# Split weights with a low half by GpSimd, in place of unsplit weights, for twelve projection tiles a layer

## The chip, the cores and the metric

The kernel runs on one core of a Trainium2 chip. The time is the device time of one execution in microseconds (us), lower is better. Matrices are multiplied by TensorE, elementwise work is done by VectorE, ScalarE and GpSimd, and the weights are read from device memory by transfers that the queue of SyncE issues.

## The reference

Two blocks of a network run one after the other, each of two layers, on 256 tokens of width 1024 in fp32. The first block's layer is

```
z = rmsnorm(x) @ w_in + b_in         # val, glu, gates, pool input, q, k, v, indexer q and k
conv  = silu(layernorm(depthwise 31-tap conv(val * sigmoid(glu)))) @ pw
pool  = windowed means of pin, mixed by small matrices
attn  = softmax over the top 64 keys an indexer picks, per query, 8 heads of 64
y     = concat(conv, pool, attn) * silu(gates)
x     = x + y @ w_out                # then a gated per-layer embedding
```

The second block (gated linear attention, short convolution, neighbourhood attention, a feed-forward part of width 2816, on 256 tokens and 256 context tokens) takes most of the time; the change doesn't touch it.

## The kernel before

**Weights.** All large weights come as a stream of units of 128x1024 fp32, in the order of use, each by one transfer into a ring `RAWB` of four slots (L457). A product in full fp32 precision is mostly made of three products of reduced precision: ScalarE writes the rounded high half of a unit into `WHI` (L1488), VectorE writes the rest, `RAWB - WHI`, into `WLO` (L2092), both rings of `SPL` = 3. TensorE's `fm` then does, for each of the eight 128x128 slabs, high weight by high x, high weight by low x, low weight by high x (L590 to L592): 24 products of 128x128 weights and 256 tokens a tile. Both engines convert units two ahead of use (`AHEAD`): in each tile's step they first convert the unit of the tile two further on and then go to the tile's own work.

**The stretch in question.** In each layer of the first block 25 projection tiles (`TILES1`) follow each other. Tiles 0 to 12 are done as told. Tiles 13 to 24 (`kb`, `pin`, `agate`, `cgate`, `pgate`) are "native" before the change: `native` (L596 to L609) multiplies the fp32 slot of `RAWB` as it is by the fp32 normalised x in `Y1`. One such product is two instructions in the trace, so a tile is 16 of them (L606). These units are not split: `NATIVE` marks them, `split_to` of ScalarE and VectorE passes over them, `SPLIT_NO` and `SPLIT_W` number the others, and the slot of `RAWB` is free when TensorE is done with it (`unit_done`).

**What lies beside these tiles.** The order on each engine is written out by hand; every engine runs its own program and waits for the others on semaphores. While the tiles go through TensorE, VectorE does rotations (`rope`), the selection of the 64 keys by repeated maxima (`topk`), the 31 taps of the convolution (`taps`, L2315, in pairs of two channel halves, after each pair a wait on its own semaphore), and per attention item (`attend`, eight items from tile 14 on) a masked maximum of each of two heads (L2338), a negation (L2342) and a reciprocal (L2348). ScalarE adds the bias on the way out of the bank (`Z`), takes the exponentials, scales them and copies the turned weights (`PT`). TensorE makes scores, turns the weights and multiplies them by the values after each tile's products. At tile 23 TensorE takes the convolution's channel mean (L1066), which needs all taps; VectorE's subtraction of it (L2359), ScalarE's square and the variance follow.

**GpSimd** does nearly nothing in this block: some transfers of its own (one, the context, waits for tile 17's eviction) and waits.

Of the kernel before, what the change touches and what calls it, by code (L numbers as in the profile page):

```python
# [19 lines left out]
F32 = mybir.dt.float32  # L20
F32R = mybir.dt.float32r
ALU = mybir.AluOpType
# [4 lines left out]
P = 128  # L27
# [19 lines left out]
    ["pin"] * 2 + ["agate"] * 4 + ["cgate"] * 2 + ["pgate"] * 2  # L47
Z1 = {n: TILES1.index(n) for n in TILES1}
NZ1 = len(TILES1)
NATIVE_FROM = Z1["kb"]  # L50
ATTEND_FROM = 14
ROPES1 = (("kiwi", 1), ("qi", 2), ("qa", 2), ("ka", 2), ("qb", 2), ("kb", 2))
ROTATE_AT = {2: 0, 3: 1, 9: 2, 11: 3, 13: 4, 15: 5}
# [73 lines left out]


def stream():
    widths, native, beside = [], [], []  # L130

    def add(ws, unsplit=False):
        widths.extend(ws)
        native.extend([unsplit] * len(ws))

    def rows(units):
        beside.extend([(len(widths) + AHEAD, ROW)] * units)

    def dots(units):
        beside.extend([(len(widths) + AHEAD, DOT)] * units)  # L140

    for l in range(DEPTH):
        add([UNIT] * 4)
        for t in range(NZ1):
            add([UNIT], t >= NATIVE_FROM)
            rows(2 if t in ROWS1 else 0)
        add([UNIT] * (2 + KS + KS))
    for l in range(DEPTH):
        add([2 * VGW] * 4)
        for i in range(NFIRST):  # L150
            add([UNIT])
            dots(DOTS_PROJ[i] if l == 0 else 0)
        for j, width in enumerate([2 * VW] * 4 + [UNIT] * (NZ2 - NFIRST)):
            add([width])
            dots(DOTS_PROJ[NFIRST + j] if l == 0 and NFIRST + j < len(DOTS_PROJ) else 0)
        rows(ROW_U if l == 0 else 0)
        for m in range(KS):
            add([UNIT])
            dots(DOTS_OUT[m] if l == 0 else 0)
        for m in range(2 * FT):  # L160
            add([UNIT])
            dots(l == 0 and m in DOTS_UP)
        for m in range(KS):
            add([UNIT, UNIT, 6 * P])
            dots(DOTS_DOWN[m] if l == 0 else 0)
    order = []
    for w in range(len(widths)):
        order.extend([kind for at, kind in beside if at == w] + [w])
    return widths, native, order


WIDTHS, NATIVE, ORDER = stream()
NW, NU = len(WIDTHS), len(ORDER)
W_AT = [ORDER.index(w) for w in range(NW)]
R_AT = [u for u in range(NU) if ORDER[u] == ROW]
D_AT = [u for u in range(NU) if ORDER[u] == DOT]
DOT_N = [2 if t < ROW_TILES + 4 else 1 for t in DOT_TILES for _ in range(4)]
DOTTED = [sum(DOT_N[:k]) for k in range(len(D_AT) + 1)]
SPLIT_W = [w for w in range(NW) if not NATIVE[w]]
SPLIT_NO = [sum(not x for x in NATIVE[:w]) for w in range(NW)]  # L180


def layout(names):
# [13 lines left out]
def build(nc, ws, prm, crep, cc, c1, c2, xt, ptin, mat1, wgp, nab, out):  # L197
    with ExitStack() as ctx:
# [234 lines left out]
        @block.sync  # L433
        def _(sp):

            def load_x(k):

                sp.dma_start(X[:, 2 * k:2 * k + 2, 0:T], xt[:, 2 * k:2 * k + 2, 0:T]).then_inc(S(f"ld_x{k}"), 16)

            load_x(0)  # L440
            for u in range(NU):
                if u in (1, 2):
                    load_x(u + u - 1)
                    if u == 1:
                        load_x(2)
                if u >= RAW:
                    w = ORDER[u - RAW]
                    if w == DOT:
                        sp.wait_ge(S("dot_summed"), DOTTED[D_AT.index(u - RAW) + 1])
                    elif w == ROW:  # L450
                        sp.wait_ge(S("row_done"), R_AT.index(u - RAW) + 1)
                    elif NATIVE[w]:
                        sp.wait_ge(S("unit_done"), w + 1)
                    else:
                        sp.wait_ge(S("lo_ready"), SPLIT_NO[w] + 1)
                n = UNIT if ORDER[u] < 0 else WIDTHS[ORDER[u]]
                sp.dma_start(RAWB[:, u % RAW, 0:n], ws[u, :, 0:n]).then_inc(S(f"raw{u % RAW}"), 16)  # L457
            for k in range(0, KS, 2):
                sp.wait_ge(S("x_new"), KS * (DEPTH + 1) + k + 2)
                sp.dma_start(out[:, k:k + 2, :], X[:, k:k + 2, 0:T]).then_inc(S("stored"), 16)  # L460
            sp.wait_ge(S("stored"), 16 * KS // 2)
# [3 lines left out]
        def _(pool):  # L465
# [6 lines left out]
            for l in range(DEPTH):  # L472
                if l > 0:
                    pool.wait_ge(S("x_new"), me.nth("x_new", KS))
                if l == 0:
                    pool.wait_ge(S("ms_ready"), 1)
                pool.dma_start(M1[:], mat1[l]).then_inc(S("ld_p1"), 16)
                pool.dma_start(PIN[:], ptin[l]).then_inc(S("ld_p1"), 16)
                if l == 0:
                    pool.dma_start(K1[:], c1).then_inc(S("ld_c1"), 16)  # L480
                    pool.wait_ge(S("ld_prm"), 16)
                nc.gpsimd.tensor_tensor(PB[:], prm_col(f"poolb{l}", 0, 2), prm_col(f"pools{l}", 0, 2), ALU.mult).then_inc(S("pb_ready"), 1)
                pool.wait_ge(S("z_freed"), NZ1 * l + 18)
                if l == 0:
                    pool.dma_start(X[:, :, T:TC], xt[:, :, T:TC]).then_inc(S("ld_ctx"), 16)
                pool.wait_ge(S("z_freed"), NZ1 * (l + 1))
            me.seen["z_freed"] = NZ1 * DEPTH
            pool.wait_ge(S("x_split"), me.nth("x_split", KS * DEPTH))
# [45 lines left out]
        def _(pe):  # L534
# [8 lines left out]
            def unit():  # L543

                u = me.u
                me.u += 1
                k = SPLIT_NO[u]
                pe.wait_ge(S("lo_ready"), k + 1)
                return WHI[:, k % SPL, :], WLO[:, k % SPL, :]

            def rows(b, s0=0, s1=KS, at=0, tiles=1):

# [23 lines left out]
            def fm(slabs, n, rhs, freed, given=None, given_from=0, order=None, b=None):  # L576

                b = me.next_tile() if b is None else b
                if b in held:
                    pe.wait_ge(*held[b])  # L580
                o = bank[b][:, 0:n]
                order = list(order or range(slabs))
                for i, s in enumerate(order):
                    if i % 8 == 0:
                        hi, lo = unit()
                    if given is not None and i >= given_from:
                        pe.wait_ge(S(given), me.nth(given))
                    w = slice((s % 8) * P, (s % 8 + 1) * P)
                    xh, xl = rhs(s)
                    nc.tensor.matmul(o, hi[:, w], xh, start=(i == 0), stop=False)  # L590
                    nc.tensor.matmul(o, hi[:, w], xl, start=False, stop=False)  # L591
                    ins = nc.tensor.matmul(o, lo[:, w], xh, start=False, stop=(i == slabs - 1))  # L592
                    if i % 8 == 7 and i != slabs - 1:
                        ins.then_inc(S("unit_done"), 1)
                ins.then_inc(S("unit_done"), 1)
                read_by(b, freed)  # L596

            def native(b, freed):

                if b in held:  # L600
                    pe.wait_ge(*held[b])
                u = W_AT[me.u]
                me.u += 1
                pe.wait_ge(S(f"raw{u % RAW}"), 16 * (u // RAW + 1))
                for s in range(KS):
                    ins = nc.tensor.matmul(bank[b][:, 0:T], RAWB[:, u % RAW, s * P:(s + 1) * P], Y1[:, s, :],  # L606
                                           start=(s == 0), stop=(s == KS - 1))
                ins.then_inc(S("unit_done"), 1)
                read_by(b, freed)  # L609

# [320 lines left out]
            for l in range(DEPTH):  # L931
# [165 lines left out]
                for t in range(NZ1):  # L1097
                    b = t % 4 if t < ATTEND_FROM - 1 else t % 2
                    if t < UNDIVIDED:
                        fm(KS, T, x_lat, "zr_ready", b=b)  # L1100
                        made["z_freed"] = made.get("z_freed", 0) + 1
                    elif t < NATIVE_FROM:
                        fm(KS, T, x_new, "z_freed", "x_split" if t == UNDIVIDED else None, b=b)
                    else:
                        native(b, "z_freed")
                    if t in ROWS1:
                        i = ROWS1.index(t)
                        pe.wait_ge(S("c_ready"), 1)
# [374 lines left out]
        def _(act):  # L1483
# [6 lines left out]
            def split_to(n):  # L1490

                nonlocal split
                while split < min(n, NW):
                    u, k, w = W_AT[split], SPLIT_NO[split], WIDTHS[split]
                    split += 1
                    if NATIVE[split - 1]:
                        continue
                    act.wait_ge(S(f"raw{u % RAW}"), 16 * (u // RAW + 1))
                    if k >= SPL:
                        act.wait_ge(S("unit_done"), SPLIT_W[k - SPL] + 1)  # L1500
                    A(WHI[:, k % SPL, 0:w], RAWB[:, u % RAW, 0:w]).then_inc(S("hi_ready"), 1)

            def rest(n=1):
# [574 lines left out]
        def _(dve):  # L2078
# [4 lines left out]
            def split_to(n):  # L2083

                nonlocal split
                while split < min(n, NW):
                    u, k, w = W_AT[split], SPLIT_NO[split], WIDTHS[split]
                    split += 1
                    if NATIVE[split - 1]:
                        continue  # L2090
                    dve.wait_ge(S("hi_ready"), k + 1)
                    V.tensor_tensor(WLO[:, k % SPL, 0:w], RAWB[:, u % RAW, 0:w], WHI[:, k % SPL, 0:w].bitcast(F32),  # L2092
                                    ALU.subtract).then_inc(S("lo_ready"), 1)
# [1082 lines left out]
```

## Time and profile before

| | us |
|---|---|
| runs of the kernel | 1410.52, 1406.16, 1413.89 (median 1410.52) |
| the profiled execution | 1411.34 |
| its span, first to last instruction | 1409.5 |
| TensorE busy | 1360.2 |
| VectorE busy | 1033.9 |
| ScalarE busy | 709.9 |
| GpSimd busy | 49.8 |

The mean granted clock of TensorE is 0.988 of full speed. All times of rows are microseconds from the start of the span unless marked ns. A busy time counts overlapping instructions once; TensorE's products are pipelined, so that one product's duration is longer than the distance to the next. An engine can be busy all the time without being what ends last, and the other way round.

### The profile page before, as it was taken

To read this page: it belongs to the slowest core of one execution; us is meant where nothing else is said; L and a number is where in the kernel's file an instruction comes from. 1 tells how busy PE (TensorE), PEld (TensorE's weight loads), DVE (VectorE), ACT (ScalarE), POOL (GpSimd) and SP (SyncE) were. 2 spreads that over 40 slices of the span, in tenths; PEclk is the share of its full clock that TensorE was granted. 3 is DMA by queue.
4 is the path that set the end of the run, shared out by engine and by line. 5 is a ranking of instruction groups with operands and counts; after the bars stand their busy time and mean duration, and the time that the engine had idled before them with its cause. 6 is when DMAs were issued, how large, how long until landed. Compare 5 with 4: busy or idle time off the path is not lost.

```text
span 1409.5 us, 21836 instructions
## 1 busy us (share of the span) xinstructions
PE 1360.2 (96%) x8477; PEld 1174.1 (83%) x8477; DVE 1033.9 (73%) x1951; ACT 709.9 (50%) x1205; POOL 49.8 (4%) x69
## 2 busy tenths in 40 slices
PE   6999999999999999999999999999999988999997
PEld 5777997879988886677888888888889877999997
DVE  6597786988679875766788888766653855788854
ACT  6536666367555632644443444322355645666643
POOL 1000000000010012000000000000000110000000
PEclk9999999999999999998999999999999999999999
DMA  7633556425456522141455544577533432455553
GB/s 262 233 133 112 189 183 219 141 91 179 154 191 195 165 90 102 50 137 57 136 160 166 164 153 154 175 265 249 162 117 105 135 105 67 139 185 180 180 193 107
DMA packets 61655, 217.73 MB, mean 154 GB/s; under 512 B 6992, under 2 KB 9040, under 8 KB 61168
## 3 DMA queue, kind: packets, MB, share of 16 engines
q1 hardware_dynamic: 58912, 204.76, 44.0%
q0 software_dynamic: 2496, 11.56, 2.4%
q8 instruction: 68, 1.11, 0.3%
q14 instruction: 35, 0.29, 0.1%
q10 hardware_dynamic: 144, 0.00, 0.0%
HBM read 215.25 MB, written 1.05 MB: 153 GB/s over the span
## 4 chain that ended last, share of the span: by engine, by line
PE 85%; ACT 6%; DVE 5%; issue 2%; DMA 1%; DVEq 0%; SPq 0%; ACTq 0%
PE bank L590 20%; PE bank L592 20%; PE bank L591 20%; PE bank L606 5%; ACT WHI L1488 2%; PE bank L1293 2%; DVE WLO L2092 1%; PE bank L651 1%; PE bank L653 1%; PE bank L652 1%; PE bank L628 1%; PE bank L629 1%; PE bank L630 1%; DMA RAWB<-in_ws 1%; PE bank L1435 1%
## 5 line engine op out<-in xcount | busy, mean ns | idle before, releaser
L590 PE MATMUL bank<-NHI,WHI 128*128 128x256 f32 (+1 forms) x1376 | 456.3, 332 | 7.7 <-DVE WLO L2092 6.0
L2092 DVE TENSOR_TENSOR WLO<-RAWB,WHI 128x1024 fp32r<-128x1024 f32 (+2 forms) x274 | 326.4, 1194 | 172.0 <-ACT WHI L1488 171.4
L591 PE MATMUL bank<-NLO,WHI 128*128 128x256 f32 (+1 forms) x1376 | 450.4, 327 | 0.0
L592 PE MATMUL bank<-NHI,WLO 128*128 128x256 f32 (+1 forms) x1376 | 450.4, 327 | 0.0
L1488 ACT ACTIVATE WHI<-RAWB 128x1024 fp32r<-128x1024 f32 (+2 forms) x274 | 281.7, 1031 | 175.6 <-PE bank L592 94.6
L590 PEld LDWEIGHTS bank<-NHI,WHI 128*128 128x128 f32 x1376 | 261.4, 190 | 39.4 <-issue 8.3
L591 PEld LDWEIGHTS bank<-NLO,WHI 128*128 128x128 f32 x1376 | 261.6, 190 | 23.7 <-issue 1.4
L592 PEld LDWEIGHTS bank<-NHI,WLO 128*128 128x128 f32 x1376 | 261.5, 190 | 22.7
L2187 DVE CUSTOM_DVE_ANT_0 DP<-RAWB,CREP,PRM 128x1024 f32<-128x1024 f32 x120 | 153.9, 1282 | 7.1 <-DMA RAWB<-in_ws 1.8
L1488 ACT ACTIVATE CF<-bank,PRM 128x512 f32<-128x512 f32 (+1 forms) x88 | 59.2, 673 | 179.3 <-PE bank L592 176.3
L590 PE MATMUL bank<-HHI,WHI 128*128 128x256 f32 (+1 forms) x330 | 109.4, 331 | 0.2 <-DVE WLO L2092 0.2
L592 PE MATMUL bank<-HHI,WLO 128*128 128x256 f32 (+1 forms) x330 | 109.3, 331 | 0.0
L591 PE MATMUL bank<-HLO,WHI 128*128 128x256 f32 (+1 forms) x330 | 109.3, 331 | 0.0
L606 PE MATMUL bank<-Y,RAWB 128*128 128x256 f32 x384 | 88.2, 383 | 0.0
L2918 DVE SCALAR_TENSOR_TENSOR CF<-bank,PRM,CF 128x510 f32<-128x510 f32 (+1 forms) x88 | 54.1, 615 | 46.3 <-ACT CF L1488 44.9
L606 PEld LDWEIGHTS bank<-Y,RAWB 128*128 128x128 f32 x384 | 71.5, 190 | 11.8 <-issue 2.7
L590 PEld LDWEIGHTS bank<-HHI,WHI 128*128 128x128 f32 x330 | 61.8, 187 | 7.6 <-DVE WLO L2092 0.4
L591 PEld LDWEIGHTS bank<-HLO,WHI 128*128 128x128 f32 x330 | 61.8, 187 | 7.1
L592 PEld LDWEIGHTS bank<-HHI,WLO 128*128 128x128 f32 x330 | 61.8, 187 | 7.1
L1488 ACT ACTIVATE L<-L,ST 128x256 f32<-128x256 f32 (+2 forms) x100 | 50.2, 517 | 31.0 <-DVE ST L2205 15.1
L1488 ACT ACTIVATE ZB<-bank 128x512 f32<-128x512 f32 (+1 forms) x34 | 17.4, 513 | 79.3 <-PE bank L592 79.2
L2921 DVE SCALAR_TENSOR_TENSOR CF<-bank,PRM,CF 128x510 f32<-128x510 f32 (+1 forms) x88 | 54.2, 616 | 3.1
(360 smaller groups left out, 1990.3 us busy)
## 6 DMA issues: line engine op xcount, KB each, us to landing
RAWB<-in_ws SPq DMA_DIRECT2D x362, 512.0 KB, 3.4
RAWB<-in_ws SPq DMA_DIRECT2D x24, 384.0 KB, 3.9
RAWB<-in_ws SPq DMA_DIRECT2D x8, 416.0 KB, 3.2
NB<-in_nab POOLq DMA_DIRECT2D x12, 256.0 KB, 3.4
CREP<-in_crep POOLq DMA_DIRECT2D x2, 1024.0 KB, 5.1
K<-in_c POOLq DMA_DIRECT2D x2, 896.0 KB, 5.6
K<-in_c POOLq DMA_DIRECT2D x1, 1344.0 KB, 8.6
X<-in_xt SPq DMA_DIRECT2D x4, 256.0 KB, 5.4
```

The lines of the kernel that those rows point to most:

```text
L590: nc.tensor.matmul(o, hi[:, w], xh, start=(i == 0), stop=False)
L591: nc.tensor.matmul(o, hi[:, w], xl, start=False, stop=False)
L592: ins = nc.tensor.matmul(o, lo[:, w], xh, start=False, stop=(i == slabs - 1))
L606: ins = nc.tensor.matmul(bank[b][:, 0:T], RAWB[:, u % RAW, s * P:(s + 1) * P], Y1[:, s, :], start=(s == 0), stop=(s == KS - 1))
L628: nc.tensor.matmul(o, hi[:, w], xh, start=(i == 0), stop=False)
L629: nc.tensor.matmul(o, hi[:, w], xl, start=False, stop=False)
L1293: ins = nc.tensor.matmul(bank[b][key_rows(j, c), c * P:(c + 1) * P], keys(j, c, 2 * seqs)[:, i, :], QD[:, i % 2, j, c * P:(c + 1) * P], st ...
L1488: return nc.scalar.activation(out, in_, func, **kw)
L2092: V.tensor_tensor(WLO[:, k % SPL, 0:w], RAWB[:, u % RAW, 0:w], WHI[:, k % SPL, 0:w].bitcast(F32), ALU.subtract).then_inc(S("lo_ready"), 1)
L2187: V.tensor_tensor_reduce(out=prod[:], in0=RAWB[:, u % RAW, :], in1=rep[:, c, :], scale=1.0, scalar=prm_col(f"bada{l}", at), op0=ALU.mult, ...
L2918: V.scalar_tensor_tensor(y[:, :, 1:], b[:, :, :-1], prm_col(f"fw{l}", j), y[:, :, 1:], ALU.mult, ALU.add).then_inc(S("dve_chain"), 1)
L2921: V.scalar_tensor_tensor(y[:, :, :-1], b[:, :, 1:], prm_col(f"fw{l}", 4 * FT + j), y[:, :, :-1], ALU.mult, ALU.add).then_inc(S("up_freed"), 1)
```

## The change

The twelve tiles a layer go through `fm` with split weights like the others. Their high halves are made by ScalarE, their low halves by GpSimd instead of VectorE. `NATIVE`, `SPLIT_NO`, `SPLIT_W` and `native` go away; every unit now takes a place in the rings `WHI` and `WLO`, and every slot of `RAWB` is free when the low half is made.

```diff
-NATIVE_FROM = Z1["kb"]
+POOL_FROM = Z1["kb"]
...
@@ SyncE's queue
-                    elif NATIVE[w]:
-                        sp.wait_ge(S("unit_done"), w + 1)
                     else:
-                        sp.wait_ge(S("lo_ready"), SPLIT_NO[w] + 1)
+                        sp.wait_ge(S("lo_ready"), w + 1)
...
@@ GpSimd
-                pool.wait_ge(S("z_freed"), NZ1 * l + 18)
-                if l == 0:
-                    pool.dma_start(X[:, :, T:TC], xt[:, :, T:TC]).then_inc(S("ld_ctx"), 16)
+                first = BY_POOL.index(True) if l == 0 else len(BY_POOL) - BY_POOL[::-1].index(True) - NZ1 + POOL_FROM
+                for k in range(first, first + NZ1 - POOL_FROM):
+                    if k == first + 20 - POOL_FROM:
+                        pool.wait_ge(S("z_freed"), NZ1 * l + 18)
+                        if l == 0:
+                            pool.dma_start(X[:, :, T:TC], xt[:, :, T:TC]).then_inc(S("ld_ctx"), 16)
+                    pool.wait_ge(S("lo_ready"), k)
+                    pool.wait_ge(S("hi_ready"), k + 1)
+                    nc.gpsimd.tensor_tensor(WLO[:, k % SPL, :], RAWB[:, W_AT[k] % RAW, :], WHI[:, k % SPL, :].bitcast(F32),
+                                            ALU.subtract).then_inc(S("lo_ready"), 1)
...
@@ TensorE
-                    elif t < NATIVE_FROM:
+                    else:
                         fm(KS, T, x_new, "z_freed", "x_split" if t == UNDIVIDED else None, b=b)
-                    else:
-                        native(b, "z_freed")
...
@@ ScalarE, split_to
-                    if NATIVE[split - 1]:
-                        continue
                     act.wait_ge(S(f"raw{u % RAW}"), 16 * (u // RAW + 1))
                     if k >= SPL:
-                        act.wait_ge(S("unit_done"), SPLIT_W[k - SPL] + 1)
+                        act.wait_ge(S("unit_done"), k - SPL + 1)
...
@@ VectorE, split_to
-                    if NATIVE[split - 1]:
+                    if BY_POOL[k]:
                         continue
+                    if k > 0 and BY_POOL[k - 1]:
+                        dve.wait_ge(S("lo_ready"), k)
                     dve.wait_ge(S("hi_ready"), k + 1)
```

## Rows read from the trace of the kernel before

**Rows 1.** The page: busy times and instructions, and the chain by engine.
```profile
PE 1360.2 (96%) x8477; PEld 1174.1 (83%) x8477; DVE 1033.9 (73%) x1951; ACT 709.9 (50%) x1205; POOL 49.8 (4%) x69
PE 85%; ACT 6%; DVE 5%; issue 2%; DMA 1%; DVEq 0%; SPq 0%; ACTq 0%
```
**Rows 2.** TensorE's timeline: start, duration, instructions.
```profile
63.46 0.39 PE L590 MATMUL bank<-NHI,WHI 128*128 128x256 f32 x1
...
66.44 1.02 PE L955 MATMUL bank<-Z,K 128*128 128x512 f32 x2
...
102.36 3.62 PE L606 MATMUL bank<-Y,RAWB 128*128 128x256 f32 x16
105.91 0.70 PE L993 MATMUL bank<-Z 64*128 64x256 f32 x4
...
134.52 1.13 PE L1066 MATMUL bank<-CV,CST 128*128 128x256 f32 x4
```
**Rows 3.** VectorE's timeline, in brackets the idle time before.
```profile
72.32 0.68 DVE L2268 TENSOR_TENSOR RT<-bank,K 128x512 f32<-128x512 f32 x1
72.92 0.68 DVE L2270 TENSOR_TENSOR Z<-Z,K 128x512 f32<-128x512 f32 x1
...
102.32 0.29 DVE L2338 CUSTOM_DVE_ANT_0 L<-bank,MB 128x128 f32<-128x128 f32 x1
...
102.94 0.87 DVE L2315 SCALAR_TENSOR_TENSOR CV<-UP,PRM,CV 128x256 f32<-128x256 f32 x2
104.05 0.17 DVE L2348 RECIPROCAL ST<-ST 128x2 f32<-128x2 f32 x1 [0.23 <-ACT L L1488]
...
106.86 0.42 DVE L2338 CUSTOM_DVE_ANT_0 L<-bank,MB 128x256 f32<-128x256 f32 x1
...
107.75 0.87 DVE L2315 SCALAR_TENSOR_TENSOR CV<-UP,PRM,CV 128x256 f32<-128x256 f32 x2
109.07 0.17 DVE L2348 RECIPROCAL ST<-ST 128x2 f32<-128x2 f32 x1 [0.45 <-ACT L L1488]
109.15 2.70 DVE L2315 SCALAR_TENSOR_TENSOR CV<-UP,PRM,CV 128x256 f32<-128x256 f32 x6
111.88 0.42 DVE L2338 CUSTOM_DVE_ANT_0 L<-bank,MB 128x256 f32<-128x256 f32 x1
...
126.11 6.36 DVE L2315 SCALAR_TENSOR_TENSOR CV<-UP,PRM,CV 128x256 f32<-128x256 f32 x14
```
**Rows 4.** Waits between 78 and 140 us (total, times, longest); one conversion by ScalarE.
```profile
ACT Z L1488 <- PE bank L606: 14.7, 8, 3.8
DVE L L2338 <- PE bank L993: 2.0, 2, 1.5
...
67.02 1.05 ACT L1488 ACTIVATE WHI<-RAWB 128x1024 fp32r<-128x1024 f32 x1
```
**Rows 5.** GpSimd's copies (ns min/median/max), the first one, VectorE beside and after.
```profile
L515 POOL COPY GQ<-EQ x24: 499/606/2489, 497.7 to 1115.5; 32x384 f32<-32x384 f32 x24
...
1109.32 2.49 POOL L515 COPY GQ<-EQ 32x384 f32<-32x384 f32 x1 [21.19 <-DVE EQ L2726]
...
1108.76 2.35 DVE L2092 TENSOR_TENSOR WLO<-RAWB,WHI 128x1024 fp32r<-128x1024 f32 x2
...
1111.99 0.63 DVE L2668 SCALAR_TENSOR_TENSOR ZB<-ZB,PRM 128x255 f32<-128x255 f32 x1
...
1113.84 1.94 DVE L2740 SCALAR_TENSOR_TENSOR EK<-EK,ZB 128x64 f32<-128x64 f32 x4
1115.70 1.52 DVE L2092 TENSOR_TENSOR WLO<-RAWB,WHI 128x1024 fp32r<-128x1024 f32 x1
...
1118.04 0.48 DVE L2668 SCALAR_TENSOR_TENSOR ZB<-ZB,PRM 128x255 f32<-128x255 f32 x1
...
1119.42 1.03 DVE L2740 SCALAR_TENSOR_TENSOR EK<-EK,ZB 128x256 f32<-128x256 f32 x4
1120.39 1.23 DVE L2092 TENSOR_TENSOR WLO<-RAWB,WHI 128x1024 fp32r<-128x1024 f32 x1
```

More of the change, by code:

```diff
@@ L129, in stream, with add @@
 def stream():
-    widths, native, beside = [], [], []
-    def add(ws, unsplit=False):
+    widths, by_pool, beside = [], [], []
+    def add(ws, low_by_pool=False):
         widths.extend(ws)
-        native.extend([unsplit] * len(ws))
+        by_pool.extend([low_by_pool] * len(ws))
     def rows(units):
@@ L144, in stream @@
         for t in range(NZ1):
-            add([UNIT], t >= NATIVE_FROM)
+            add([UNIT], t >= POOL_FROM)
             rows(2 if t in ROWS1 else 0)
@@ L168, in stream @@
         order.extend([kind for at, kind in beside if at == w] + [w])
-    return widths, native, order
-WIDTHS, NATIVE, ORDER = stream()
+    return widths, by_pool, order
+WIDTHS, BY_POOL, ORDER = stream()
 NW, NU = len(WIDTHS), len(ORDER)
@@ L178 @@
 DOTTED = [sum(DOT_N[:k]) for k in range(len(D_AT) + 1)]
-SPLIT_W = [w for w in range(NW) if not NATIVE[w]]
-SPLIT_NO = [sum(not x for x in NATIVE[:w]) for w in range(NW)]
 def layout(names):
@@ L546, in unit @@
                 me.u += 1
-                k = SPLIT_NO[u]
-                pe.wait_ge(S("lo_ready"), k + 1)
-                return WHI[:, k % SPL, :], WLO[:, k % SPL, :]
+                pe.wait_ge(S("lo_ready"), u + 1)
+                return WHI[:, u % SPL, :], WLO[:, u % SPL, :]
             def rows(b, s0=0, s1=KS, at=0, tiles=1):
@@ L594, in fm @@
                         ins.then_inc(S("unit_done"), 1)
[L595 to L607, printed above, removed]
                 ins.then_inc(S("unit_done"), 1)
@@ L1493, in split_to @@
                 while split < min(n, NW):
-                    u, k, w = W_AT[split], SPLIT_NO[split], WIDTHS[split]
+                    u, k, w = W_AT[split], split, WIDTHS[split]
                     split += 1
-                    if NATIVE[split - 1]:
-                        continue
                     act.wait_ge(S(f"raw{u % RAW}"), 16 * (u // RAW + 1))
                     if k >= SPL:
-                        act.wait_ge(S("unit_done"), SPLIT_W[k - SPL] + 1)
+                        act.wait_ge(S("unit_done"), k - SPL + 1)
                     A(WHI[:, k % SPL, 0:w], RAWB[:, u % RAW, 0:w]).then_inc(S("hi_ready"), 1)
@@ L2086, in split_to @@
                 while split < min(n, NW):
-                    u, k, w = W_AT[split], SPLIT_NO[split], WIDTHS[split]
+                    u, k, w = W_AT[split], split, WIDTHS[split]
                     split += 1
-                    if NATIVE[split - 1]:
+                    if BY_POOL[k]:
                         continue
+                    if k > 0 and BY_POOL[k - 1]:
+                        dve.wait_ge(S("lo_ready"), k)
                     dve.wait_ge(S("hi_ready"), k + 1)
```

## The prediction

> **What bounds the kernel now.** I read the chain of waits first. TensorE holds 85% of it, VectorE 5%, and GpSimd is busy 4% of the span [rows 1]. That invites the short answer: make TensorE's tiles shorter and the kernel is shorter. So I went to the timeline of the changed stretch, the tiles 13 to 24 of one layer of the first block (78.8 to 139 us; layer 1 repeats it some 183 us later with the same durations).
>
> TensorE is nearly without a gap there. The reader is to see two distances in the start times [rows 2]: a split tile starts at 63.46 and its successor operation at 66.44, so it takes 2.98 us (24 products); an unsplit tile takes from 102.36 to 105.91, 3.55 us (16 products). A split tile is thus about 0.6 us shorter, though it has more products.
>
> Then VectorE over the same stretch [rows 3]. One item of attention is there: two masked maxima, a convolution tap pair, a short wait of 0.45 us for the exponentials, the reciprocal, three more tap pairs, and at 111.88 the next item. It waits for TensorE's scores only twice in the stretch, 2.0 us in all, 1.5 of it before one late item [rows 4]; until that item it has been at work since about 71 us (rotations, the selection's maxima, taps). Its taps end at 132.47 (126.11 + 6.36). TensorE's channel mean, which needs them, starts at 134.52. So VectorE is behind TensorE by a slack that is small: 2.05 us at the end, and 2.0 us inside. Everything that TensorE wins in the stretch beyond 4.0 us a layer finds VectorE late. That is the limit of the gain, and also the cover of any loss on VectorE.
>
> **The change part by part.**
>
> 1. TensorE: 24 tiles (12 a layer) are 0.6 us shorter: 14.4 us off TensorE. Up to the channel mean 11 tiles of a layer, 6.6 us, count. VectorE lets at most 4.0 of them through. The twelfth lies beside the chain channel mean, subtraction, square on the other engines, and brings nothing.
>
> 2. ScalarE: 24 more conversions of 1.05 us [rows 4], one a tile from tile 11's place in the program on, two tiles ahead of use. Each stands before ScalarE's wait for the tile's products. It waited there in 8 of the tiles, 14.7 us in all; so the conversion lies in that wait. For an item with 256 keys ScalarE would have two exponentials (1.1), two scalings (0.9), conversion (1.0), eviction (0.4), copy of the turned weights (0.5) and 0.4 us of waiting for the reciprocal: 4.3 of VectorE's 5.02 us (106.86 to 111.88). Cost nothing; if that cover were gone, at most 0.5 us a tile.
>
> 3. DMA queue: the twelve slots are freed by the subtraction, two tiles earlier than by the products. Loads of the same size start earlier; nothing. GpSimd's load of the context now stands between subtractions, and its wait (tile 17's eviction) comes before the conversion of tile 20 in ScalarE's order, so it holds nothing up. The ring of three converted tiles is now shared by the tiles 22 to 24 and the next units: the third of these, converted ahead in one go, must wait for tile 24's products, which end about when ScalarE gets there. At most 0.5 us; I take nothing. VectorE's added wait before its first own unit is for a subtraction made a tile earlier.
>
> 4. GpSimd: 24 subtractions of 128x1024 with two inputs. No such row exists. Its copies of 32x384 elements take 0.50 to 0.61 us when little disturbs them [rows 5], fastest and median, so 1.3 to 1.6 ns an element read; 2048 elements read make 2.7 to 3.2 us. Even that is under the tile's 5 us, and there are two tiles to do it in. GpSimd's own time is no limit.
>
> 5. What it does to VectorE. This decides the sign. Rows 5 show the only place where GpSimd reads SBUF while VectorE works. The first copy starts at 1109.32 when VectorE has back-to-back subtractions of two SBUF tiles: they take 2.35 us for two, undisturbed, and the copy ends only at 1111.81 (2.49 us instead of 0.50). From then on VectorE's two-input operations are the longer ones: 0.63 instead of 0.48, four products with a quarter of the elements 1.94 instead of 1.03, and a subtraction 1.52 instead of 1.23. With the others of the stretch some 1.8 us over eight copies: 0.22 us a copy, at most 0.30. So the two engines exclude each other, GpSimd gets in where VectorE pauses for a semaphore of its own, and VectorE then stands. A tap pair ends with such a pause, each.
>
> The Trainium skill says the same more strictly (SBUF — State Buffer, Who interferes with whom): a VectorE instruction with two SBUF inputs and a GpSimd instruction that reads SBUF share an interface, and whichever is second "fully blocks" for the whole instruction. The stretched rows agree in direction; that a long subtraction would hold it to its end, no row here can show. GPSIMD Engine Reference, Elementwise — side-by-side cycle accounting, measures 4497 ns for a two-input fp32 operation of 2048; half of it, 2.25 us, would by the sum below make +24 us.
>
> Price of one subtraction to a VectorE that wants the interface: from below 0.22 us per 384 elements read, 2048 read, 1.2 us; from above the copy's whole time, 3.2 us. If the engines didn't exclude each other at all it would be 0. I take 1.9, between the two, near the copy's fastest time less its start and end.
>
> Not all of it is felt: VectorE's operations with one SBUF input go on. Where would GpSimd start? ScalarE's conversion ends about 2.1 us after a reciprocal (0.3 wait, 0.8 scalings, 1.0), in the third tap pair; so GpSimd gets in at its end, and beside it run the two maxima, which read a bank (0.62 us to the next tap for 128 keys, 0.89 for 256 [rows 3]). Then the tap stands; the wait for exponentials behind it (0.23 or 0.45) takes up some. Cover so 0.85 us for tiles 18 and 19, 1.34 for 20 to 23. Tile 17's subtraction has maxima and the rotation's first product, 1.3. For tiles 13 to 16 VectorE is in rotations and the selection's maxima. Laid against its order by where their conversions would end (72, 77, 80 and 83 us, shifted by what went before) I estimate 0.6 (the first product of a rotation reads a bank, the second doesn't [rows 3]), 0.4, 1.4 (four one-input searches) and 0. Tile 24's falls in the last fourteen taps: 0. Sum of cover 10.8 us.
>
> Sum a layer: 12 x 1.9 = 22.8, less 10.8, VectorE is 12.0 us later; less 4.0 of slack and waits, the channel mean is 8.0 us later. Behind it the chain (subtraction, square, root, projections) is the old one. Two layers: +16 us. The profiled execution took 1411.3 (span 1409.5), so 1427.3; the median shown is 0.8 below it, so I say 1427. TensorE, though shorter in each tile, gets gaps of 1 to 2 us in the tiles.
>
> **Rivals.**
> - A, on the other side: the engines don't exclude each other for these operations, or for a negligible time. Then VectorE alone is the limit, and 2 x 4.0 are won: 1403. It holds in sign while a subtraction costs VectorE less than about 1.1 us, where the felt parts (only tiles 13, 14, 16, 18, 19 and 24 have less cover) sum to the slack. For it: the stretch of rows 5 is some tenths. Against: the same rows have it in nearly each two-input operation.
> - B, TensorE is the limit throughout, as the chain's 85% have it: 14.4 us less, 1397. Against it stands VectorE's continuous work.
> - C, exclusion at the upper price: 12 x 3.2 - 10.8 - 4.0 = 23.6 a layer, 1458. The rule quoted lies between at 1436. For it: the block may hold longer than GpSimd's reading.
> - D, price at its lower end, 1.2: felt 4.5, less 4.0, twice: +1, 1412.
> - E, the low parts come late and TensorE waits for GpSimd instead: a subtraction would have to last over 5 us. Then 24 x (its time - 5); at 6 us +24. No row makes it likely.
>
> **How the numbers follow.** Forecast with prices between 1.5 and 2.6 us (1417 to 1445): 0.57. A 0.10, B 0.03, C 0.13 beyond 1445, D 0.14, E 0.03. The range to hold eight in ten: 1403 to 1450. About 0.5% (7 us) is what a measurement of this kernel tells from no change. A at -8 is just faster, in part same; so faster 0.11, same 0.15, slower 0.74.
>
> **What would show it.** Right: taps of 0.45 us of which one an item takes about 2 us; VectorE's busy time (not its work) up by 20 us or more in the two stretches; waits of TensorE for VectorE's or ScalarE's attention results; channel mean later by some 8 us a layer; tile products 2.98 us; nothing changed behind the first block. Wrong: taps undisturbed (A), or waits of the products for the low halves (E). The main risk is the one price with no row of its own.

## The result, and the profile after

The changed kernel takes 1446.6 us, median of four runs (1443.58 to 1450.67), against 1409.77 us of the kernel before in the same series (four runs, 1406.16 to 1413.89). The ratio is 1.0264, with an interval of 1.0244 to 1.0284: 36.8 us slower. Forecast were 16 us slower, 1427. The sign and the mechanism came as forecast; the size did not. The profiled execution took 1443.58 us with a span of 1441.8.

The page of the changed kernel: busy times, and the chain that ended last, by engine (it answers to [rows 1]).
```profile
PE 1354.8 (94%) x8669; PEld 1178.4 (82%) x8669; DVE 1078.1 (75%) x1951; ACT 730.0 (51%) x1229; POOL 108.6 (8%) x93
PE 73%; DVE 16%; ACT 7%; issue 3%; DMA 1%; SPq 0%; DVEq 0%; ACTq 0%
```
VectorE has the same 1951 instructions and is busy 44.2 us longer. Its share of the chain went from 5% to 16%, TensorE's from 85% to 73%.

VectorE's groups by line and form in both layers of the first block, first of the kernel before (70 to 350 us), then of the changed one (70 to 360 us): busy us and mean ns of one, then idle time.
```profile
L2315 DVE SCALAR_TENSOR_TENSOR CV<-UP,PRM,CV 128x256 f32<-128x256 f32 x120 | 52.5, 479 | 1.2
L2270 DVE TENSOR_TENSOR Z<-Z,K 128x512 f32<-128x512 f32 x9 | 6.1, 681 | 0.0
L2342 DVE TENSOR_SCALAR ST<-ST 128x2 f32<-128x2 f32 x16 | 2.7, 169 | 0.6
L2313 DVE TENSOR_SCALAR CV<-UP,PRM 128x256 f32<-128x256 f32 x4 | 1.5, 410 | 0.1
```
```profile
L2302 DVE SCALAR_TENSOR_TENSOR CV<-UP,PRM,CV 128x256 f32<-128x256 f32 x120 | 74.0, 658 | 1.2
L2257 DVE TENSOR_TENSOR Z<-Z,K 128x512 f32<-128x512 f32 x9 | 9.8, 1085 | 0.0
L2329 DVE TENSOR_SCALAR ST<-ST 128x2 f32<-128x2 f32 x16 | 11.6, 722 | 0.6
L2300 DVE TENSOR_SCALAR CV<-UP,PRM 128x256 f32<-128x256 f32 x4 | 7.1, 1826 | 0.1
```
The work is the same, the durations are not, and the idle time of these groups has not moved. VectorE, held up by GpSimd, shows it here as long instructions, not as waits. Two of the four groups have one input only: the negation of the two maxima (a scaling of 128x2) and the first tap.

GpSimd in the changed kernel: its 24 subtractions, min/median/max ns.
```profile
L487 POOL TENSOR_TENSOR WLO<-RAWB,WHI x24: 2339/2398/2625, 71.2 to 346.0; 128x1024 fp32r<-128x1024 f32 x24
```
VectorE's and GpSimd's timelines of the changed kernel, layer 0: start, duration, engine.
```profile
71.63 2.50 DVE L2257 TENSOR_TENSOR Z<-Z,K 128x512 f32<-128x512 f32 x1
...
76.40 2.15 DVE L2300 TENSOR_SCALAR CV<-UP,PRM 128x256 f32<-128x256 f32 x2
...
97.36 1.87 DVE L2329 TENSOR_SCALAR ST<-ST 128x2 f32<-128x2 f32 x1
...
103.08 3.03 DVE L2302 SCALAR_TENSOR_TENSOR CV<-UP,PRM,CV 128x256 f32<-128x256 f32 x2
...
107.96 4.84 DVE L2302 SCALAR_TENSOR_TENSOR CV<-UP,PRM,CV 128x256 f32<-128x256 f32 x6
...
125.35 1.49 DVE L2329 TENSOR_SCALAR ST<-ST 128x2 f32<-128x2 f32 x1
...
141.69 8.53 DVE L2302 SCALAR_TENSOR_TENSOR CV<-UP,PRM,CV 128x256 f32<-128x256 f32 x14
151.51 0.69 DVE L2346 TENSOR_TENSOR CV<-CV,bank 128x512 f32<-128x512 f32 x1 [1.29 <-PE bank L1055]
```
```profile
109.92 2.59 POOL L487 TENSOR_TENSOR WLO<-RAWB,WHI 128x1024 fp32r<-128x1024 f32 x1 [4.09 <-ACT WHI L1475]
124.47 2.35 POOL L487 TENSOR_TENSOR WLO<-RAWB,WHI 128x1024 fp32r<-128x1024 f32 x1 [5.26 <-ACT WHI L1475]
...
143.87 2.41 POOL L487 TENSOR_TENSOR WLO<-RAWB,WHI 128x1024 fp32r<-128x1024 f32 x1 [3.52 <-ACT WHI L1475]
```
A tap pair lasts 0.87 us when nothing disturbs it, and 3.03 here; six taps 2.70, and 4.84 here; fourteen 6.36, and 8.53. The difference is 2.15 us each time. The Trainium skill has a rule for this (SBUF — State Buffer, Who interferes with whom): a VectorE instruction of two SBUF inputs and a reading GpSimd instruction lock each other out for whole instructions. The trace agrees, with a stop somewhat shorter than the subtraction: 2.15 us stand beside one of 2.34 to 2.62. The Trainium skill's GPSIMD Engine Reference, Elementwise — side-by-side cycle accounting, gives 4497 ns for 2048 elements; its half, 2.25 us, an estimate, is slightly under what GpSimd took here for 1024.

I measure both kernels on one distance, from VectorE's first product of the third of the six rotations (72.32 before, 71.03 after) to the subtraction of the channel mean (135.75 before, 151.51 after). Before it is 63.4 us in layer 0 and 63.7 in layer 1; after, 80.5 and 82.9. That is 17.1 + 19.2 = 36.2 us, which fits the 36.8 between the medians. The two profiled executions differ by less, 32.3 us of span: the changed one came to the first stretch 1.3 us earlier and was 2.6 us shorter behind the second. The experiments below use this distance and call it the stretch.

TensorE in the changed kernel, timeline around the scores of the second item of attention, and the windows around it (us, then busy time of PE, PEld, DVE, ACT, POOL, then granted clock, DMA share, GB/s).
```profile
93.72 0.49 PE L982 MATMUL bank<-Z 64*128 64x128 f32 x4 [3.29 <-DVE ST L2325]
95.59 0.68 PE L994 MATMUL bank<-CST,L 128*128 128x128 f32 x2 [1.38 <-ACT L L1475]
95.92 0.56 PE L592 MATMUL bank<-NHI,WHI 128*128 128x256 f32 x1
96.28 0.41 PE L593 MATMUL bank<-NLO,WHI 128*128 128x256 f32 x1
96.49 0.41 PE L594 MATMUL bank<-NHI,WLO 128*128 128x256 f32 x1
```
```profile
89.00:96.00 7.00, 2.33 (x14) 1.32 (x13) 6.39 (x21) 1.83 (x7) 0.00 (x0) 0.88 0.00 0
96.00:101.30 5.30, 5.30 (x27) 5.10 (x26) 5.06 (x12) 2.19 (x7) 2.38 (x1) 0.51 0.20 46
101.30:106.00 4.70, 4.43 (x35) 3.70 (x34) 4.56 (x8) 2.27 (x5) 2.54 (x1) 1.00 0.15 62
```
TensorE now waits for VectorE's maxima. After gaps of 3.3 and 1.4 us the products start 0.21 us apart instead of 0.12: the granted clock is 0.51, the lower of its two levels (1.2 of 2.4 GHz). One tile of 24 products is 2.2 us longer by it. That adds nothing to the loss that VectorE's row shows: VectorE did not wait for TensorE here, and the time that it stood accounts for the stretch alone (below).

### The profile page after: what moved, and what is told of

Same layout as the page of the kernel before. It is cut to its first block, busy times and chain, and to the rows that moved or that the text cites. A ratio compares the mean times of both kernels' runs of the same rounds, so it can differ in the third digit from the quotient of the medians.

```text
span 1441.8 us, 22313 instructions
## 1 busy us (share of the span) xinstructions
PE 1354.8 (94%) x8669; PEld 1178.4 (82%) x8669; DVE 1078.1 (75%) x1951; ACT 730.0 (51%) x1229; POOL 108.6 (8%) x93
## 4 chain that ended last, share of the span: by engine, by line
PE 73%; DVE 16%; ACT 7%; issue 3%; DMA 1%; SPq 0%; DVEq 0%; ACTq 0%
PE bank L592 19%; PE bank L594 19%; PE bank L593 19%; DVE CV L2302 4%; ACT WHI L1475 2%; ACT L L1475 2%; PE bank L1280 1%; DVE WLO L2079 1%; PE bank L640 1%; PE bank L642 1%; PE bank L641 1%; PE bank L617 1%; DVE SC L2286 1%; PE bank L618 1%; PE bank L619 1%
## 5 line engine op out<-in xcount | busy, mean ns | idle before, releaser
L592 PE MATMUL bank<-NHI,WHI 128*128 128x256 f32 (+1 forms) x1568 | 517.7, 330 | 7.7 <-DVE WLO L2079 6.0
L593 PE MATMUL bank<-NLO,WHI 128*128 128x256 f32 (+1 forms) x1568 | 507.8, 324 | 0.0
L594 PE MATMUL bank<-NHI,WLO 128*128 128x256 f32 (+1 forms) x1568 | 507.5, 324 | 0.0
L1475 ACT ACTIVATE WHI<-RAWB 128x1024 fp32r<-128x1024 f32 (+2 forms) x298 | 306.9, 1032 | 184.1 <-PE bank L594 99.7
L592 PEld LDWEIGHTS bank<-NHI,WHI 128*128 128x128 f32 x1568 | 301.5, 192 | 42.7 <-issue 11.1
L593 PEld LDWEIGHTS bank<-NLO,WHI 128*128 128x128 f32 x1568 | 301.7, 192 | 24.6 <-issue 2.2
L594 PEld LDWEIGHTS bank<-NHI,WLO 128*128 128x128 f32 x1568 | 301.5, 192 | 22.5
L2302 DVE SCALAR_TENSOR_TENSOR CV<-UP,PRM,CV 128x256 f32<-128x256 f32 x120 | 74.0, 658 | 1.2
L487 POOL TENSOR_TENSOR WLO<-RAWB,WHI 128x1024 fp32r<-128x1024 f32 x24 | 58.6, 2441 | 201.0 <-DVE WLO L2079 107.9
L592 PEld LDWEIGHTS bank<-HHI,WHI 128*128 128x128 f32 x330 | 61.8, 187 | 7.5 <-DVE WLO L2079 0.4
L594 PEld LDWEIGHTS bank<-HHI,WLO 128*128 128x128 f32 x330 | 61.8, 187 | 7.2
L593 PEld LDWEIGHTS bank<-HLO,WHI 128*128 128x128 f32 x330 | 61.8, 187 | 7.1
```

What stands on the lines that cost most here:

```text
L487: nc.gpsimd.tensor_tensor(WLO[:, k % SPL, :], RAWB[:, W_AT[k] % RAW, :], WHI[:, k % SPL, :].bitcast(F32), ALU.subtract).then_inc(S("lo_rea ...
L1475: return nc.scalar.activation(out, in_, func, **kw)
L2302: ins = V.scalar_tensor_tensor(CV[:, m, :], src, w, CV[:, m, :], ALU.mult, ALU.add)
```

## The experiments

**No subtraction.** The first question is whether the twelve subtractions or the rest of the change cost the time. GpSimd only clears two columns of each low part and signals; the low parts are missing from the sums, everything else stays.
```diff
-  nc.gpsimd.tensor_tensor(WLO[:, k % SPL, :], RAWB[...], WHI[...].bitcast(F32), ALU.subtract)
+  nc.gpsimd.memset(WLO[:, k % SPL, 0:2].bitcast(F32), 0.0)
```


> The changed kernel with GpSimd's 24 subtractions left out: in their place it writes two columns of WLO, so the low halves of these weights are missing and the output is not the reference's. Everything else of the change stays (24 conversions on ScalarE, split products, waits, ring). Theory (GpSimd's reading shuts VectorE out, 2.15 us each): VectorE undisturbed, only the limit of VectorE is left, 2 x 4.0 us faster than before: about 1402. Rival 1 (conversions on ScalarE, the shared ring or the added waits make the loss): stays near 1440. Rival 2 (the products' lower clock makes the loss): gaps of TensorE go too, so 1402 as well, told apart by the idle subtractions' run.

Measured: 1402.15 us (six runs), ratio 0.9949 (0.9929 to 0.9969). The stretch is 59.5 and 59.8 us, 4.0 and 3.9 less than before: exactly the limit that VectorE's slack sets. Its groups are back at the old durations:
```profile
L2301 DVE SCALAR_TENSOR_TENSOR CV<-UP,PRM,CV 128x256 f32<-128x256 f32 x120 | 52.5, 479 | 1.2
```
So the conversions on ScalarE, the freed loads and the wait at GpSimd's context load cost nothing that is seen, and the twelve split tiles could give 6 to 8 us in the two layers. All of the loss, and these as well, goes to the subtraction: 44.5 us between the medians over 24, or 1.85 each.

**Writes without reads.** Is it GpSimd's reading that locks, or its time on SBUF at all? In place of the subtraction two clearings, of a spare tile and of the low part (so again without low parts), for about the same time together.
```diff
-  nc.gpsimd.tensor_tensor(WLO[...], RAWB[...], WHI[...].bitcast(F32), ALU.subtract)
+  nc.gpsimd.memset(SPARE[:, 0:1600], 0.0)
...                        # the second clearing waits for the first
+  nc.gpsimd.memset(WLO[:, k % SPL, :].bitcast(F32), 0.0)
```


> As the run without subtraction, but GpSimd writes without reading for about as long as a subtraction takes (1600 columns of a spare tile, then the 1024 of WLO, together some 2.3 us by the rate of its memsets, 0.87 ns a column); the low halves are missing. Theory as I hold it (VectorE is shut out by GpSimd's reads alone): the same as without subtraction, about 1402, except that negations and scalings that VectorE runs at its double rate may be stopped by writes. Rival (any GpSimd access shuts VectorE out): near the changed kernel, 1440.

Measured: 1406.93 us (ten runs), ratio 0.9987 (0.9973 to 1.0001). The groups of VectorE, and of GpSimd:
```profile
L2304 DVE SCALAR_TENSOR_TENSOR CV<-UP,PRM,CV 128x256 f32<-128x256 f32 x120 | 52.5, 484 | 1.2
...
L2331 DVE TENSOR_SCALAR ST<-ST 128x2 f32<-128x2 f32 x16 | 7.1, 446 | 0.6
```
```profile
L488 POOL MEMSET SPARE<- 128x1600 f32 x24 | 34.5, 1436 | 165.4 <-DVE WLO L2081 108.4 <-ACT WHI L1477 57.0
L490 POOL MEMSET WLO<- 128x1024 f32 x24 | 22.9, 953 | 1.4
```
GpSimd is at work for 2.39 us each time, as long as for a subtraction, and the 120 taps are untouched: it is the reads that hold up a tap. The other row is the exception that the expectation left open. The negation of two columns, one input, goes from 168 to 446 ns on the mean. It is held in another way than beside a subtraction, as VectorE's timeline shows:
```profile
107.46 0.87 DVE L2331 TENSOR_SCALAR ST<-ST 128x2 f32<-128x2 f32 x1
107.53 0.87 DVE L2304 SCALAR_TENSOR_TENSOR CV<-UP,PRM,CV 128x256 f32<-128x256 f32 x2
109.56 0.17 DVE L2337 RECIPROCAL ST<-ST 128x2 f32<-128x2 f32 x1 [1.15 <-ACT L L1477]
```
The tap pair starts 0.07 us behind the negation and keeps its 0.87, so VectorE doesn't stand; only the end of the negation comes late. ScalarE's exponentials wait for that end, and VectorE then waits for them, here 1.15 us instead of 0.45. Over both layers VectorE's waits before the reciprocals are 8.4 us instead of 5.4; that is most of the 3.6 us by which the stretches (61.1 and 61.8) are above those of the last kernel. The medians differ by 4.8. This small instruction needs something that GpSimd's writes occupy too, and the two-input taps don't.

**One input.** GpSimd copies the unsplit part instead of subtracting (the low part then holds the weight itself).
```diff
-  nc.gpsimd.tensor_tensor(WLO[...], RAWB[...], WHI[...].bitcast(F32), ALU.subtract)
+  nc.gpsimd.tensor_copy(WLO[:, k % SPL, :], RAWB[:, W_AT[k] % RAW, :])
```


> The changed kernel with a GpSimd copy of the weights into WLO in place of the subtraction: one tensor read instead of two, so the low halves are not what the reference wants. Theory (VectorE stands for as long as GpSimd reads): the copy of 1024 takes 1.0 to 1.4 us, VectorE stands about 1.0 each, less cover some 6 to 9 a layer, less 4.0: 1412 to 1420. Rival (a fixed price per GpSimd instruction): 1440 as in the changed kernel.

Measured: 1411.85 us (eight runs), ratio 1.0034 (1.0022 to 1.0045). GpSimd's copy, and taps of VectorE beside one and beside none:
```profile
L487 POOL CAST WLO<-RAWB 128x1024 fp32r<-128x1024 f32 x24 | 26.9, 1122 | 199.6 <-DVE WLO L2078 108.2 <-ACT WHI L1474 91.5
```
```profile
105.49 3.48 DVE L2301 SCALAR_TENSOR_TENSOR CV<-UP,PRM,CV 128x256 f32<-128x256 f32 x6
...
111.30 2.70 DVE L2301 SCALAR_TENSOR_TENSOR CV<-UP,PRM,CV 128x256 f32<-128x256 f32 x6
```
VectorE stands 0.79 us; the copy beside this row runs from 107.45 and takes 1.25 us, the mean of all 24 is 1.12. One input of 1024 costs 0.79, two inputs 2.15: 2.7 times, not twice. An extrapolation by elements read, as I made it from the copies of [rows 5], is too low for that reason among others: its rate would give 0.6 us for this copy. The stretches are 64.8 and 65.2 us. The time is 9.7 us over the kernel with no subtraction, 0.40 each, and just under the 1412 to 1420 expected.

**The subtractions alone.** The reverse of the first: the kernel before, with its unsplit tiles, and 24 subtractions on a spare tile that nothing else reads, released by the evictions and the finished items. The edit is shown shortened.
```diff
+  for t in range(11, 23):
+      pool.wait_ge(...)   # z_freed for 4, p_ready for 8
+      nc.gpsimd.tensor_tensor(SPARE[:, 0, :], SPARE[:, 0, :], SPARE[:, 1, :], ALU.subtract)
```


> The kernel before, with unsplit products, and twelve GpSimd subtractions a layer on a spare tile that nobody uses, four released by evictions 10 to 13, eight by the scaled exponentials of the items. Theory: VectorE is stopped for 1.3 to 2.15 us by each, 16 to 25 a layer, less 4.0 of slack: 12 to 21 a layer, 1434 to 1452, as slow as the changed kernel though no product, conversion or ring was touched. Rival (the loss is in conversions, ring or waits, or in the products): 1410.

Measured: 1447.91 us (four runs), ratio 1.0281 (1.0256 to 1.0306): as slow as the changed kernel, without one change to TensorE's work. The stretch is 81.0 us in layer 0 and 81.2 in layer 1; the first subtraction of layer 0 (71.34 us) lies ahead of it.
```profile
L2327 DVE SCALAR_TENSOR_TENSOR CV<-UP,PRM,CV 128x256 f32<-128x256 f32 x120 | 77.7, 689 | 1.2
```
Together with the first experiment this closes the matter of the cause: take the subtraction away and the loss is gone, put only it in and the loss is there.

**VectorE subtracts.** If the subtraction must stand on somebody, what does it cost on VectorE itself, 1.23 us each [rows 5]?
```diff
@@ GpSimd
-  nc.gpsimd.tensor_tensor(WLO[...], RAWB[...], WHI[...].bitcast(F32), ALU.subtract)
@@ VectorE, split_to
-  if BY_POOL[k]:
-      continue          # VectorE leaves these low parts to GpSimd
```


> The 24 subtractions made by VectorE itself, as for all other units; GpSimd makes none. Theory: VectorE pays 12 x 1.15 = 13.8 us a layer of its own work in place of 21 of standing, less 4.0 of slack: 9.8 a layer, about 1430, and faster than the changed kernel by 14. Rival (moving work off VectorE did help, loss is elsewhere): slower than the changed kernel by up to 2 x 13.8.

Measured: 1429.71 us (four runs), ratio 1.0153 (1.013 to 1.0177), about the 1430 expected. The stretch is 73.0 in both layers. Twelve times 1.15 to 1.2 us less 4.0 of slack is +10; measured is +9.5. VectorE doing the work itself loses a little over half of what it loses by letting GpSimd do it (18.9 us in the two stretches against 36.2), since a subtraction of its own takes 1.2 us where GpSimd's stops it for up to 2.15.

**The negation in two halves.** In the changed kernel the negation of two columns stands in three items a layer, for 1.3 to 1.9 us. Here it is written as two instructions of one column.
```diff
-  V.tensor_scalar(ST1[:, s, 1, :], ST1[:, s, 0, :], -HD ** -0.5, None, ALU.mult)
+  for e in range(2):
+      V.tensor_scalar(ST1[:, s, 1, e:e + 1], ST1[:, s, 0, e:e + 1], -HD ** -0.5, None, ALU.mult)
```


> The changed kernel with the negation of the two maxima made as two instructions of one column instead of one of two columns, so that it can't run at the double rate. Theory: this negation no longer stands (0.17 instead of 1.3 to 1.9 us in three items a layer); the tap behind it stands instead, but beside ScalarE's exponentials: 1 to 2 us a layer less, near 1441. Rival (the negation stands for its own read, whatever its rate): lengths as in the changed kernel, 1.3 to 1.9.

Measured: 1445.46 us, one run. VectorE's timeline:
```profile
98.59 0.22 DVE L2330 TENSOR_SCALAR ST<-ST 128x1 f32<-128x1 f32 x2
98.72 0.68 DVE L2255 TENSOR_TENSOR RT<-bank,K 128x512 f32<-128x512 f32 x1
99.32 1.67 DVE L2257 TENSOR_TENSOR Z<-Z,K 128x512 f32<-128x512 f32 x1
...
126.16 2.02 DVE L2302 SCALAR_TENSOR_TENSOR CV<-UP,PRM,CV 128x256 f32<-128x256 f32 x2
```
One column is not held up; the next operation with two SBUF inputs stands instead, 1.0 us at 99.32 and 1.15 at 126.16, less by what passed in between. The stretch is 1.5 and 1.2 us shorter, near the 1 to 2 us a layer expected; the total, expected near 1441, is not, but a single run can't show it. So the negation is mostly the first that meets the lock. What its place adds is that the exponentials wait for it: when the tap behind it stands instead, they run beside it, and the wait of 0.45 us before the reciprocal is gone.

**Three, beside the searches.** If the lock is what costs, subtractions placed beside VectorE's searches of the selection (the repeated maxima, one input) should be free. Only tiles 15, 16 and 17 are split, and GpSimd waits for the place. ScalarE converts tile 17 one tile earlier (not shown).
```diff
+BY_POOL_AT = (15, 16, 17)
+  pool.wait_ge(S(gate), count)   # VectorE's causal mask, fifth rotation, first reciprocal
+  nc.gpsimd.tensor_tensor(WLO[...], RAWB[...], WHI[...].bitcast(F32), ALU.subtract)
```


> From the kernel before: only tiles 15, 16 and 17 of a layer on split weights (tiles 13, 14, 18 to 24 stay unsplit), their low halves by GpSimd, each released by a semaphore so that it runs beside VectorE's searches of the maxima, which have one SBUF input and run at the single rate: the first after the causal addition of the second half, the second after the fourth rotation, the third after the first reciprocal. The conversion for tile 17 is made one tile earlier. Theory (only two-input and double-rate operations stand): VectorE's operations keep their lengths, TensorE wins 3 x 0.6 a layer: 3.6 us less than before, 0.9974. Rival (any subtraction costs VectorE 2.15): 3 x 2.15 less 4.0 of slack, 2.4 us a layer later: 4.9 us more than before.

Measured: 1406.22 us (twelve runs), ratio 0.9981 (0.9972 to 0.9989). GpSimd, and VectorE beside it:
```profile
84.79 2.39 POOL L492 TENSOR_TENSOR WLO<-RAWB,WHI 128x1024 fp32r<-128x1024 f32 x1 [2.85 <-DVE Z L2288]
```
```profile
84.66 0.43 DVE L2312 MAX8 M<-SC 128x8 f32<-128x256 f32 x1
85.12 0.09 DVE L2314 MATCH_VALUE_LOAD SC<-M,SC 128x8 f32 x1
85.20 0.41 DVE L2314 MATCH_REPLACE8 SC<-M,SC 128x256 f32<-128x256 f32 x1
```
The searches keep their durations beside a whole subtraction: where VectorE runs nothing that takes the lock, the subtraction is free. The stretch is 0.8 and 0.7 us shorter, not the 1.8 of three tiles. TensorE, now earlier, stops for the last rotation, which the scores of the third item need, and for the weights of the second, waits that it did not have:
```profile
93.14 0.49 PE L1004 MATMUL bank<-Z 64*128 64x128 f32 x4 [0.17 <-DVE Z L2288]
93.93 0.53 PE L1016 MATMUL bank<-CST,L 128*128 128x128 f32 x2 [0.29 <-ACT L L1499]
```

**And tile 13 by VectorE.** To the last kernel tile 13 is added, its low part by VectorE itself.
```diff
-  add([UNIT], t >= NATIVE_FROM and t not in BY_POOL_AT)
+  add([UNIT], t > NATIVE_FROM and t not in BY_POOL_AT)
```


> As the three in the searches, and tile 13 on split weights as well, its low half by VectorE (1.15 us of the 4.0 of slack). Theory: TensorE wins 4 x 0.6 = 2.4 a layer, VectorE would allow 2.85: 4.8 us less than before, 0.9966, the fastest that runs the whole computation. Rival (VectorE's slack is smaller than 4.0 or is spent): no better than the three.

Measured: 1409.86 us (eleven runs), ratio 1.0003 (0.9992 to 1.0013). A miss: 0.9966 was expected. The stretch is 63.8 and 63.7, 1.1 and 0.8 longer than without tile 13, and TensorE's wait for the weights of the first item, at 91.25 us, is now 1.15 us, where the kernel without tile 13 had none. Early in the stretch VectorE has no slack: its 1.2 us go straight to the first items.

**And two late ones by VectorE.** In place of tile 13, tiles 22 and 23. Their subtractions fall before the seventh and eighth item, where VectorE waited for scores [rows 4].
```diff
+BY_VECTOR_AT = (22, 23)
-  add([UNIT], t >= NATIVE_FROM and t not in BY_POOL_AT)
+  add([UNIT], t >= NATIVE_FROM and t not in BY_POOL_AT + BY_VECTOR_AT)
```


> The three tiles in the searches, and besides tiles 22 and 23 on split weights with their low halves by VectorE. Theory: the run with three won only 0.8 a layer because VectorE's fifth rotation and the second item's weights stop TensorE at item 2; VectorE's waits of 1.5 and 0.47 us lie later, before items 6 and 7, where the two subtractions of 1.15 would fall. TensorE wins 1.2 a layer more, VectorE has 0.3 more to do than wait: 2 x 2.0 = 4 us less than before, 0.9972. Rival (VectorE is the limit in the late part too): as the three alone or slower, 0.998 to 1.000.

Measured: 1403.68 us (eleven runs, 1402.12 to 1406.82) against 1408.72, ratio 0.9966 (0.9954 to 0.9979): this version is 5 us below the kernel before, and the fastest that runs the whole computation. The stretch is 61.7 in both layers, 1.7 and 2.0 less.
```profile
116.28 1.23 DVE L2108 TENSOR_TENSOR WLO<-RAWB,WHI 128x1024 fp32r<-128x1024 f32 x1
117.43 0.42 DVE L2354 CUSTOM_DVE_ANT_0 L<-bank,MB 128x256 f32<-128x256 f32 x1
```
The subtraction ends and the masked maximum follows with no wait for scores: it took the place of the idle time. VectorE's idle time in the stretch falls from 10.4 to 6.4 us in layer 0, so the slack of 4.0 is used up: 2.3 of it by the two subtractions, 1.7 by the shorter stretch.

**The two late ones alone.** Tiles 22 and 23 added to the kernel before, nothing by GpSimd.
```diff
-  add([UNIT], t >= NATIVE_FROM)
+  add([UNIT], t >= NATIVE_FROM and t not in BY_VECTOR_AT)
```


> The kernel before with tiles 22 and 23 alone on split weights, low halves by VectorE, nothing by GpSimd. Theory: 2 x 1.2 = 2.4 us less than before, 0.9983. Rival as above: 1.000 or slower.

Measured: 1407.81 us (twelve runs), ratio 0.9995 (0.9984 to 1.0005). The stretch is 1.2 us shorter in each layer, as expected; the total, expected at 0.9983, shows some 0.7 of these 2.4 us, with an interval that reaches to 2.3. Whether anything is lost behind the stretch is open.

## Why the prediction was right in sign and short in size

- **The bound, and the slack of 4.0 us a layer: right.** With the subtraction taken out and all else left in, the stretch is 4.0 and 3.9 us shorter, though TensorE's eleven tiles are 6.6 shorter. In the changed kernel VectorE's idle time in the stretch fell by 4.0 and 3.9 us as well.
- **ScalarE, the queues, GpSimd's own time: right.** They were costed at nothing, and the same experiment shows nothing. TensorE never waited for a low part in the two stretches.
- **The exclusion: right.** VectorE's durations grew with its work unchanged, and the subtractions alone reproduce the loss.
- **"Price of one subtraction ... I take 1.9": too low.** It is 2.15. By element read, my lower bound from [rows 5] gave 1.2 and the fastest copy 2.7; between them I chose too low. That is 12 x 0.25 = 3.0 us a layer.
- **"Sum of cover 10.8 us": this is the step that failed.** Laid out one by one, VectorE stood 1.82, 1.41, 0.68, 2.00, 1.70, 2.16, 2.15, 2.15, 1.32, 2.12, 1.36 and 2.17 us in layer 0: 21.0 us, where the sum said 12.0. Of the full price 25.8, only 4.8 was covered. That is 6.0 us a layer. In layer 1 it stood 23.1 us, so only 2.7 were covered. Tiles 13 to 16 had 2.7 us of cover in layer 0 where the sum said 2.4, but 0.7 in layer 1, so the first of these is partly luck; tiles 17 to 24 had 2.1 and 2.0 where the sum said 8.4. Three assumptions were false:
  - After the third tap pair I let the maxima run beside the subtraction, to the next tap. But the negation of these maxima comes first, and it stands (1.49 us at 125.35 instead of 0.17). The exponentials wait for it, so the wait of 0.45 behind the tap took up nothing of it.
  - I let GpSimd in only where VectorE pauses for a semaphore. At 109.92 it is in the trace beside a tap that runs from 109.77 for 0.48 us, and the next tap of the same pair, which follows at once, lasts 2.63 (the row is below): it came in between two taps. So four of the eight tiles from 17 on had next to no cover at all (tiles 18, 19, 20 and 22), and tile 24 none, as forecast. The copy of [rows 5], which had waited through two long subtractions, had suggested otherwise; what decides who is let in, no run here settles. (The same section of the Trainium skill says that whichever of the two issues first holds the interface; the tap behind 109.92 agrees, the copy of [rows 5] doesn't quite, since the second subtraction went ahead of it.)
  - The taps' first product and the mask product, with one input, I counted as free. They stand too: the first product lasts 1826 ns instead of 410 in the group above. In layer 0 that took nothing from the sum. In layer 1 two of them stood one behind the other, 2.1 us each (the second row below; 0.74 undisturbed), and that is where the cover of tiles 13 to 16 went. The Trainium skill has such scalings among those that can run in a two-port mode and then contend with GpSimd (SBUF — State Buffer, Who interferes with whom); the trace agrees, and I applied the rule to two-input operations only.
```profile
110.17 2.63 DVE L2302 SCALAR_TENSOR_TENSOR CV<-UP,PRM,CV 128x256 f32<-128x256 f32 x1
...
276.12 5.00 DVE L2300 TENSOR_SCALAR CV<-UP,PRM 128x256 f32<-128x256 f32 x2
```
- **The sum.** 21.0 less 4.0 is 17.0; the stretch of layer 0 grew by 17.1. In layer 1, 23.1 less 3.9 is 19.2, and the stretch grew by 19.2. The two together, 44.1 us, are also what VectorE's busy time grew by over the whole kernel (44.2). Against the 24.0 us of the forecast that is 20.1 more: 6.0 by the price, 14.1 by the cover.
- **The tail: right as far as can be seen.** The stretch's 36.2 us and the 36.8 between the medians agree. In the two traces the part behind the second stretch is 1090.8 us before and 1088.2 after; in the traces of the experiments it is 1087.5 to 1093.2, so a change of a few us there would not be seen.
- **The rivals.** A fell with the first row of taps. B fell with the run with no subtraction, where TensorE had all its tiles and the gain stopped at VectorE's slack. E fell, since no product waited for a low part. D is excluded by the 2.15 us. C came nearest: its place and cover were wrong like mine, its result of 1458 over by 11. The 1436 that stands beside it had nearly the right price, 2.25, and falls 11 short by the cover. With 2.15 and my cover the sum gives 1433, so a right price alone would not have been enough.

## What to carry to other kernels

GpSimd is no free helper for VectorE when it reads SBUF: before moving work to it, price each such instruction at nearly its full duration on VectorE, unless VectorE at that moment runs a search, reads a bank, or waits; credit no cover that hasn't been matched instruction by instruction, small ones included. Work that VectorE does itself in 1.2 us is cheaper there than at GpSimd for 2.15 us of standing. What pays is small and placed: subtractions of GpSimd beside searches, and those of VectorE in the waits that it really has, gave 5 us where the whole move lost 37.

## What the runs showed of the hardware that I had not expected

- A two-input subtraction of 128x1024 by GpSimd (2.34 to 2.62 us) stops VectorE for 2.15 us, a one-input copy (1.25 beside a tap) for 0.79.
- GpSimd's writes alone leave VectorE's two-input taps at 484 ns, but lengthen a scaling of two columns from 168 to 446 ns on the mean. VectorE's next instruction starts on time then (0.07 us behind, the scaling lasting 0.87); only what waits for the scaling is late. Beside a subtraction the scaling takes up to 1.87 us, and the next instruction does start late. Two such scalings of one column each take 0.22 us together beside a subtraction.
- GpSimd gets in between two taps that follow each other at once: the second lasts 2.63 us instead of 0.48.
- VectorE's searches (0.43 and 0.41 us) and its masked maxima, which read a bank (0.42 at 124.54), keep their durations beside a subtraction.
- After gaps of 3.3 and 1.4 us TensorE was granted 0.51 of its clock for about 5 us of products. In the kernel before it had 1.00 throughout layer 0's stretch, where it was never idle.
